# Hybrid encoder layer on one core: the order of weight loads, x1 stores, part sums and a memset in the last stage

## The reference, cut to what matters

```
xn = rms_norm(x);  q, k, v, u, g_attn, g_ssm = split(xn @ w_in)
attn_out = attention(rope(norm(q)), rope(norm(k)), v) @ w_attn_proj
y        = gelu(s5_bidirectional(u));  ssm_out = (y @ w_glu_a) * sigmoid(y @ w_glu_b)
x1 = x + (sigmoid(g_attn) * attn_out + sigmoid(g_ssm) * ssm_out) @ w_out
h  = rms_norm(x1)
out = x1 + square(relu(h @ w_ff1)) @ w_ff2          # w_ff1 1024 x 4096, w_ff2 4096 x 1024
```

## Time and profile before

| | |
|---|---|
| time, median of 3 runs | 2521.76 us (2520.86 to 2523.23) |
| the profiled execution: its own time | 2514.49 us |
| its span, first to last instruction | 2512.7 us |
| TensorE busy | 2473.1 us, 98% |
| VectorE, ScalarE, GpSimd busy | 1681.6, 1124.3, 1081.5 us |
| part one (three blocks) | from about 1083 to 1490 us |
| part two, first half; second half | to about 2004; to 2512 us |

### The profile page before, as it was taken

How to read it: one execution, slowest core, us unless ns; L and a number is a source line. 1 busy time by engine, 2 the same in 40 slices (tenths; PEclk the granted TensorE clock), 3 DMA queues, 4 the chain that set the end, 5 groups by cost and what they waited for, 6 DMA issues and landing times.

```text
span 2512.7 us, 37695 instructions
## 1 busy us (share of the span) xinstructions
PE 2473.1 (98%) x12320; PEld 2193.9 (87%) x12320; DVE 1681.6 (67%) x2349; ACT 1124.3 (45%) x1903; POOL 1081.5 (43%) x908
## 2 busy tenths in 40 slices
PE   8999999999999999999999989999999999999999
PEld 6888888888777777778787879999999999999999
DVE  7986688888888888876676766444446854444442
ACT  7554112121777777754444444333334343333341
POOL 0005664644667666654444423333333333333332
PEclk9999999999999999999999999999999999999999
DMA  5544232324552221144555633222222332222221
GB/s 184 178 161 168 87 98 82 94 81 108 139 121 70 51 64 44 38 158 151 193 193 197 223 133 135 68 68 68 68 68 94 122 132 69 70 70 68 68 68 67
DMA packets 160221, 271.29 MB, mean 108 GB/s; under 512 B 47184, under 2 KB 63056, under 8 KB 159952
## 3 DMA queue, kind: packets, MB, share of 16 engines
q1 hardware_dynamic: 160080, 269.46, 34.1%
HBM read 200.08 MB, written 59.24 MB: 103 GB/s over the span
## 4 chain that ended last, share of the span: by engine, by line
PE 91%; DVE 3%; DMA 2%; issue 1%; ACT 1%; SPq 1%; POOL 0%; DVEq 0%; ACTq 0%; POOLq 0%
PE banks L63 14%; PE banks L65 14%; PE banks L64 14%; PE banks L2859 6%; PE banks L2856 6%; PE banks L2858 6%; PE p_acc L63 3%; PE p_acc L65 3%; PE p_acc L64 3%; PE banks L1929 3%; PE banks L1928 3%; PE banks L1882 3%; PE banks L1877 3%; PE banks L1897 3%; PE banks L1876 3%; DMA t_wraw<-w_tail_t 2%
## 5 line engine op out<-in xcount | busy, mean ns | idle before, releaser
L63 PE MATMUL banks<-block,t_whi 128*128 128x384 f32 (+1 forms) x1088 | 387.8, 356 | 8.2 <-issue 5.7
L65 PE MATMUL banks<-block,t_wlo 128*128 128x384 f32 (+1 forms) x1088 | 386.6, 355 | 0.0
L1727 POOL TENSOR_TENSOR a_plo<-a_p,a_phi 128x512 fp32r<-128x512 f32 x239 | 308.8, 1305 | 141.1 <-DVE a_phi L1845 135.4
L2638 DVE TENSOR_TENSOR f_x<-banks,f_x 128x384 f32<-128x384 f32 x256 | 142.2, 557 | 293.1 <-PE banks L65 287.7
L64 PE MATMUL banks<-block,t_whi 128*128 128x384 f32 (+1 forms) x928 | 333.0, 359 | 0.0
L2856 PE MATMUL banks<-block,t_whi 128*128 128x384 f32 x800 | 268.7, 336 | 7.3 <-ACT f_snap L2503 5.4
L2859 PE MATMUL banks<-block,t_wlo 128*128 128x384 f32 x800 | 268.1, 335 | 0.0
L2385 POOL TENSOR_TENSOR t_wlo<-t_wraw,t_whi 128x1024 fp32r<-128x1024 f32 x67 | 164.3, 2453 | 229.2 <-ACT t_whi L2406 229.2
L2858 PE MATMUL banks<-block,t_whi 128*128 128x384 f32 x768 | 257.3, 335 | 0.0
L2390 POOL TENSOR_TENSOR t_wlo<-a_quotient,t_whi 128x512 fp32r<-128x512 f32 x96 | 141.8, 1477 | 224.4 <-ACT t_whi L2421 224.4
L1772 ACT ACTIVATE a_p<-banks 128x512 f32<-128x512 f32 x320 | 190.6, 596 | 95.8 <-PE banks L1929 86.8
(11 more groups left out here) (327 smaller groups left out, 6333.8 us busy)
## 6 DMA issues: line engine op xcount, KB each, us to landing
t_wraw<-w_tail_t SPq DMA_DIRECT2D x136, 512.0 KB, 4.2
a_quotient<-w_tail_t SPq DMA_DIRECT2D x64, 512.0 KB, 3.7
block<-roped_scratch SPq DMA_DIRECT2D x144, 128.0 KB, 2.8
w_raw<-w_in_t SPq DMA_DIRECT2D x31, 512.0 KB, 4.0
proj_scratch<-s_gate SPq DMA_DIRECT2D x48, 256.0 KB, 2.1
t_graw<-proj_scratch SPq DMA_DIRECT2D x24, 512.0 KB, 3.9
p_sw<-p_qn SPq DMA_DIRECT2D x60, 128.0 KB, 2.1
roped_scratch<-p_r_hi SPq DMA_DIRECT2D x30, 256.0 KB, 2.2
```

The lines of the kernel that those rows point to most:

```text
L63: pe.matmul(out, whi, xhi, start=start, stop=False)
L65: return pe.matmul(out, wlo, xhi, start=False, stop=stop)
L1727: pool.tensor_tensor(p_lo[s][:], p32[s][:], f32(p_hi[s][:]), ALU.subtract).then_inc(plo_pool, 1)
```

## The change

Six things, all in `tail`:

- SyncE: in the output projection tile loads are issued one step earlier. `next_w(b, S_2, 0)` stands ahead of the loop over m, `next_w` of m + 1 stands at the head of step m, the first `next_w` of the next block in step 7. The stores of x1 go one step later: tiles 0 to 5 behind steps 2, 4 and 6, tiles 6 and 7 in the next block's first step (or at the end).
- SyncE, last block: stage tiles 2 and 3 are loaded in steps 1 and 3 instead of 2 and 4, with a new wait for the stage tile before; weight units 2 and 3 in steps 6 and 7 instead of after the last store.
- VectorE: `rs` is cleared ahead of the last block's output projection too, and no longer at t = 2.
- VectorE: at the last block's m = 7 the low part of item 1 goes ahead of the fourth weight sum.
- VectorE: the second half's token parts are made in two portions per item, one ahead of the first eviction and one behind it; the sums can stop after each.
- ScalarE: at the items 168 and 344 (`group_at[h, 7]`) the last pair's results are split at the head of the step.

```diff
--- before.py
+++ after.py
@@ -2288,6 +2288,8 @@
                 view = stage_at(h, kt)[:].rearrange("p (k n) -> p k n", k=2)
                 rows = lambda t, n0, n1: t[kt:kt + KH + 1:KH, :, n0:n1].rearrange("k p n -> p k n")
                 if h == 0:
+                    if kt:
+                        st_in.wait(sp, 16 * kt)
                     sp.dma_start(view, rows(normed_d, 0, HALF)).then_inc(st_in.sem, 16)
                 else:
                     sp.dma_start(view[:, :, 0:2 * BLK - HALF], rows(normed_d, HALF, 2 * BLK)).then_inc(st_in.sem, 16)
@@ -2298,14 +2300,20 @@
                 mixed.wait(sp, 16 * h + 4 * (kt + 1))
                 mixed_lo.wait(sp, mixed_count(h, kt, 2))
 
+            def store_x1(b, i):
+                sp.wait_ge(x1_ready, b * KD + 2 * i + 4)
+                sp.dma_start(two_tiles(x1_d, b, i), x1[:, 2 * i:2 * i + 2]).then_inc(x1_out.sem, 16)
+
             for b in range(NBLK):
                 for m in range(KD):
                     for s in range(2):
-                        if not (b == 0 and m == 0 and s == 0):
+                        if (m, s) != (0, 0):
                             next_w(b, 2 * m + s, s)
                     if b == 0:
                         if m < 4:
                             load_x(0, m)
+                    elif m == 0:
+                        store_x1(b - 1, KD // 2 - 1)
                     elif m >= 4:
                         hn_out.wait(sp, 16 * (4 * (b - 1) + m - 2 if m < 6 else 4 * b))
                         load_x(b, m - 4)
@@ -2319,12 +2327,16 @@
                     if b == LAST and m == KD - 2:
                         hn_out.wait(sp, 16 * 4 * LAST)
                         load_stage(0, 0)
+                next_w(b, S_2, 0)
                 if b < LAST:
                     for s in range(2):
                         sp.wait_ge(st.attention[s], 16 * (NQ * NBLK // 2))
                     mix_chunk(b + 1, 0)
                 for m in range(KD):
-                    next_w(b, S_2 + m, m % 2)
+                    if m + 1 < KD:
+                        next_w(b, S_2 + m + 1, (m + 1) % 2)
+                    elif b < LAST:
+                        next_w(b + 1, 0, 0)
                     if b < LAST:
                         if m + 1 < N_MIX + 2:
                             mix_chunk(b + 1, m + 1)
@@ -2333,14 +2345,14 @@
                         load_stage(0, 1)
                         load_unit(0)
                         load_unit(1)
-                    elif m in (2, 4):
-                        stage_free(0, m // 2 - 1)
-                        load_stage(0, m // 2 + 1)
-                    if m % 2:
-                        sp.wait_ge(x1_ready, b * KD + m + 3)
-                        sp.dma_start(two_tiles(x1_d, b, m // 2), x1[:, m - 1:m + 1]).then_inc(x1_out.sem, 16)
-            load_unit(2)
-            load_unit(3)
+                    elif m in (1, 3):
+                        stage_free(0, m // 2)
+                        load_stage(0, m // 2 + 2)
+                    elif m >= KD - 2:
+                        load_unit(m - KD + 4)
+                    if m in (2, 4, 6):
+                        store_x1(b, m // 2 - 1)
+            store_x1(LAST, KD // 2 - 1)
 
             due = {}
             for r in range(4, len(feed.last_use)):
@@ -2488,9 +2500,24 @@
                             act.wait_ge(mix_in[m % 2], (b + 1) * 48 - 48 + (m // 2 + 1) * 16)
                             act.activation(chunk(m)[1], g_raw[m % 2][:], ACT.Copy).then_inc(mixhi_ready, 1)
 
+            def split_results(t):
+
+                for pg, i in a_parts(t, 0):
+                    r, c = a_order(pg)[i]
+                    h, p = divmod(pg, FF_PAIRS)
+                    if p >= 3:
+                        act.wait_ge(f2_done, 16 * (h * 8 + (p - 3) // 2 + 1))
+                    elif h:
+                        act.wait_ge(f2_done, 16 * 8)
+                    c_done.wait(act, 7 * pg + {(0, 1): 4, (1, 1): 5, (0, 0): 6, (1, 0): 7}[r, c])
+                    act.activation(act_cell(slot_of(pg), 0, r, c), ps[:, a_bank(pg, r, c), 0:QN],
+                                   ACT.Copy).then_inc(ahi_ready, 1)
+
             for t in range(3):
                 f_high(t)
             for t in range(END + 2):
+                if t in (feed.group_at[0, 7], feed.group_at[1, 7]):
+                    split_results(t)
                 for pg, d in feed.pairs_near(t, 1, 3):
                     h = pg // FF_PAIRS
                     if d == 1:
@@ -2516,16 +2543,8 @@
                         mix_high(1, kt, c)
                 if t + 3 < END:
                     f_high(t + 3)
-                for pg, i in a_parts(t, 0):
-                    r, c = a_order(pg)[i]
-                    h, p = divmod(pg, FF_PAIRS)
-                    if p >= 3:
-                        act.wait_ge(f2_done, 16 * (h * 8 + (p - 3) // 2 + 1))
-                    elif h:
-                        act.wait_ge(f2_done, 16 * 8)
-                    c_done.wait(act, 7 * pg + {(0, 1): 4, (1, 1): 5, (0, 0): 6, (1, 0): 7}[r, c])
-                    act.activation(act_cell(slot_of(pg), 0, r, c), ps[:, a_bank(pg, r, c), 0:QN],
-                                   ACT.Copy).then_inc(ahi_ready, 1)
+                if t not in (feed.group_at[0, 7], feed.group_at[1, 7]):
+                    split_results(t)
                 if t < 2:
                     for kt in (2 * t, 2 * t + 1):
                         mix_high(0, kt, T4)
@@ -2574,10 +2593,12 @@
                 if kt or h:
                     mixed_lo.wait(dve, 28 + 7 * kt if h else 6 * kt)
                 dve.tensor_tensor(t1, b12, b11, ALU.subtract).then_inc(mixed.sem, 1)
+                yield
                 mixed.wait(dve, n + 1)
                 dve.tensor_tensor(t2, b22, t1, ALU.subtract).then_inc(mixed.sem, 1)
                 yield
                 dve.tensor_tensor(t3, b22, b12, ALU.subtract).then_inc(mixed.sem, 1)
+                yield
                 mixed.wait(dve, n + 2)
                 if h and kt == 0:
                     c_done.wait(dve, 7 * FF_PAIRS)
@@ -2672,8 +2693,7 @@
                         for k in (2 * m - 2, 2 * m - 1):
                             dve.scalar_tensor_tensor(x1[:, k], x1[:, k], gn[:, k:k + 1], rs[:], ALU.mult,
                                                      ALU.mult).then_inc(hn_ready.sem, 1)
-                if b < LAST:
-                    dve.memset(rs[:], 0.0).then_inc(sq_step, 1)
+                dve.memset(rs[:], 0.0).then_inc(sq_step, 1)
                 dve.wait_ge(const_in, 32)
                 dve.wait_ge(x1_in, 16 * 4 * (b + 1))
                 for m in range(KD):
@@ -2692,12 +2712,12 @@
                         else:
                             for c in PREP[3:6]:
                                 quarter_low(0, kt, c)
-                        if m >= KD - 4:
-                            weight_sum(0, m - KD + 4)
                         if m == KD - 1:
                             for t in range(2):
                                 if feed.on_dve(t):
                                     f_low(t)
+                        if m >= KD - 4:
+                            weight_sum(0, m - KD + 4)
                     dve.wait_ge(summed, b * M_T + S_2 + m + 3)
                     dve.tensor_tensor(x1[:, m], ps[:, O_BANK + s], x1[:, m], ALU.add).then_inc(x1_ready, 1)
                     if b < LAST:
@@ -2709,7 +2729,30 @@
 
             if feed.on_dve(2):
                 f_low(2)
-            sums_of = None
+            sums_of = {kt: quarter_sums(1, kt) for kt in range(KH)}
+
+            def scale_new(kt, i):
+
+                if i == 0:
+                    st_in.wait(dve, 16 * KH + 32 * (kt + 1))
+                    dve.wait_ge(rs_ready, NBLK)
+                new = stage_at(1, kt)[:].rearrange("p (k n) -> p k n", k=2)[:, i, 2 * BLK - HALF:]
+                k = kt + KH * i
+                dve.scalar_tensor_tensor(new, new, gn[:, k:k + 1], rs2, ALU.mult, ALU.mult).then_inc(hn_ready.sem, 1)
+
+            def prepare(at, late_half):
+
+                if not 0 <= at < 16:
+                    return
+                kt, step = divmod(at, 4)
+                sums_now, lows = ((0, 1), (2, 1), (0, 0), (0, 0))[step][late_half], (
+                    ((), ()), ((), (B11,)), ((B22, B21), (T1,)), ((T2, T3), (T4,)))[step][late_half]
+                if step == 0:
+                    scale_new(kt, late_half)
+                for _ in range(sums_now):
+                    next(sums_of[kt], None)
+                for c in lows:
+                    quarter_low(1, kt, c)
             for t in range(END + 3):
                 if 0 < t <= END and feed.items[t - 1].kind == "f2":
                     evict(t - 1, 1)
@@ -2749,36 +2792,15 @@
                 if t in (1, 2):
                     for kt in (2 * t - 2, 2 * t - 1):
                         quarter_low(0, kt, T4)
-                if t == 2:
-                    dve.memset(rs[:], 0.0).then_inc(sq_step, 1)
```

(23 more changed lines are left out.)

## The result

| | before | after |
|---|---|---|
| median (lowest to highest) | 2521.33 us (2520.86 to 2523.23), 4 runs | 2496.14 us (2495.44 to 2503.57), 4 runs |
| ratio | | 0.991, 95% interval 0.9894 to 0.9925 |
| the profiled execution: time, span | 2514.49, 2512.7 us | 2496.11, 2494.3 us |

The change takes 25 us (1.0%) off the median. The prediction was 2503, range 2499 to 2512: the direction is right, the time lies 3 us under the range. Between the two traces the difference is only 18.4 us, and 18.9 had been predicted for that. So the working by stalls came out near for the trace, and the step from the trace to the median did not hold.

What follows compares the result with a forecast made beforehand. TensorE, busy 98% of the span, was taken as the bound, so only its stalls and low clock could be won. Gains of 4.5 + 3.6 + 5.5 + 3.9 + 1.4 = 18.9 us off 2521.8 gave 2503 us, range 2499 to 2512.

Steps and rivals of the forecast that it cites:

- the step from the trace to the median: Whole kernel: the gain of 18.9 us counted in the 2514.5 us trace was taken unchanged off the 2521.8 us median.
- part 1: Ends of the three blocks' output projections: weight tiles loaded ahead of x1 stores remove stalls, 4.5 plus 3.6 us.
- The price of a stall: TensorE's stalls: each costs its bracket plus some 0.15 us; low clock behind each of two long ones, 1.5 us.
- Tiles ahead of the stores: Output projections: earlier weight tile loads gain 4.5 us in the third block, 3.6 us at the ends of blocks one and two.
- 0.4 to 0.5 us too late for m=6: Third block's output projection: VectorE's addition of m=4 would end this much too late for TensorE's m=6.
- Items 0 to 20: Stretch to the last mean: early weight units 2 and 3 and memset gain 5.5 us, VectorE becoming the bound.
- Token parts and splits: Second half's preparation in two portions gains 3.9 us; splitting the last pair's results first gains 1.4 us.
- B: Rival: VectorE takes back more, before the mean and in the token parts' late halves; 2508 us, chance 0.17.
- C: Rival: early tiles come no earlier, as transfers set the time; only 2 of 8.1 us stay; 2509 us, chance 0.08.
- D: Rival: crowded transfers make at least five of 24 tiles land over 8.7 us after issue; 2528 us, chance 0.06.

Runs made afterwards that it cites:

- memset_only: The kernel before with only the memset of `rs` moved ahead of the output projection; 2518.08 us median, ratio 0.9994 to the kernel before.
- before_again: The kernel before, unchanged, run again for a second trace; 2515.75 us median over 10 runs.
- before_b: The kernel before, unchanged, run for a further trace; that trace took 2524.73 us.
- before_c: The kernel before, unchanged, run once more for another trace; that trace took 2515.3 us.
- sp_only: The kernel before with only SyncE's new order (tiles ahead of stores, weight units 2 and 3 early); 2503.98 us median, ratio 0.9934 to the kernel before.
- no_memset: The changed kernel with only the memset of `rs` put back at t = 2; 2500.9 us median, ratio 0.992 to the kernel before.
- old_parts: The changed kernel with the second half's token parts made as before, in one portion ahead of the first eviction; 2502.19 us median.
- no_sp: The changed kernel with SyncE's whole order as before; 2511.62 us median over nine runs, ratio 0.9968 to the kernel before.

## Why the prediction was wrong in its number, and where it was right

**The step that failed** is the one from the trace to the median: "the holes are the same work, so I take the same gain from it". For the profiled execution the prediction's figure was 2495.6 us and that execution took 2496.1. The median before lay 7 us over its trace, and these 7 us were taken to stay. They did not, and could not be counted on to, for two reasons that the runs show.

First, the holes are not the same work in each execution. In the old order a weight tile is asked for so late that a landing 1.2 us longer became a stall 1.25 us longer at the first tile and 2.5 us longer at the next (memset_only), and the low clock follows some of these stalls and not others. Six traces with the old order took 406.4 to 412.1 us to item 0, 408.2 in the mean; eight with the new order took 397.3 to 398.0. The first trace, 406.5, was among the shortest. So part 1 was worth 8.5 us between the two traces (4.5 + 3.6 = 8.1 predicted) and 10.4 us in the mean.

Second, the start of the last stage has two levels, 1083 to 1085 or 1090 to 1092 us, with any of these kernels (9 traces and 5). The change does not set it, but a few runs of each kernel can fall on unequal levels.

What the change is worth apart from such draws can be had in two ways. The means of the stretches differ by 10.4 + 5.4 + 5.8 + 0.5 = 22 us. The 54 runs of the kernel before on record (with before_again, before_b and before_c) have a median of 2518.2 us, the eight of the changed kernel one of 2495.8: 22.4 us. So of the 25 us measured some 22 are the change's, where 18.9 had been taken; the other 3 are the luck of the four runs that made the median before, 3 us above the 54. No trace exists of those four, so whether their 7 us over the first trace were the later level, longer stalls or both stays open. The range should have held an execution of average length.

**Term by term**, in the two first traces:
- The price of a stall was too low. From the matmul ahead of it to the fourth behind it, each of the five late-tile stalls of the trace before takes 0.24 to 0.25 us more than its bracket and the rhythm, not 0.15; the low clock behind the one at m=4 lasted 3.4 us at 0.5, which costs 1.7 us, not 1.5.
- Tiles ahead of the stores: 8.1 predicted, 8.5 measured. The four stalls and the one at m=4 went, and "0.4 to 0.5 us too late for m=6" is the 0.49 us of the trace.
- Items 0 to 20: 5.5 predicted, 5.6 measured, and VectorE became the bound as forecast: it worked from the addition of m=6 to the last squares without a gap, 21.9 us (1482.62 to 1504.49) against the 21.7 counted. TensorE's wait for it is 3.4 us at item 6; at the mean there is none, probably as the low clock had made item 6 slower (sp_only, without it, waits 0.8 us there). no_memset shows the memset's own share to be nothing, sp_only that SyncE's order alone wins all of it.
- Token parts and splits: 3.9 + 1.4 = 5.3 predicted, 5.7 + 0.5 = 6.3 measured (5.74 + 0.53). The halves took nearly every wait away (the waits for f_x are gone from the view above, where 1.0 us had been allowed for), and the first split is worth nothing by itself.
- Upstream, the stage began 2.0 us later in the trace after, which no part of the change touches (part of it is a low clock from 638.71 to 642.12 us, which the trace before has not): 20.4 less 2.0 is the 18.4 us between the traces.

Of the rivals, B and C did not come about: nothing beyond the counted work was taken back, and the tiles did come earlier. In part one, from 1095 us on, a tile lands in 3.8 us as a median where it took 4.5. For D, crowding: the longest landing is 6.5 us, under the 8.7 at which TensorE would stop, with three transfers in each step. Where the Trainium skill was cited (SBUF — State Buffer, "Who interferes with whom"), the trace agrees in the direction it shows: the weight sum at 1487.54 takes 1.78 us beside a subtraction of GpSimd that had started at 1487.22 and lasted 1.56 us, where such a sum alone takes 0.68. That GpSimd made TensorE wait in the new order was not seen.

## What to carry to other kernels

Before a gain read from one trace is taken off a median, place that trace among the kernel's runs: where a load sits so late that its landing time is on the path, the stall's size is a draw, and the trace shows one draw. In an issue queue that runs in order, put the load that only waits for a free buffer ahead of the store that waits for the newest result. And when a long wait is taken from an engine that then has work back to back, count that work: it gave 5.6 us here where 8 us of TensorE's stalls and a low clock had stood, and it left nothing for the memset or for most of a further spreading.

## What the runs showed of the hardware

The attention stage ahead of the last one runs at two speeds with the granted clock at 1.00 in both (1.00 is 2.4 GHz, 0.50 is 1.2). From 700 to 1070 us, TensorE's busy time, count of matmuls, clock, DMA share and GB/s: first before, then sp_only.

```profile
700.00:1070.00 370.00, 369.79 (x1595) 1.00 0.26 63
```

```profile
700.00:1070.00 370.00, 369.78 (x1568) 1.00 0.25 63
```

The slower one gets 27 matmuls less done in 370 us, 1.7%, which over that loop makes the 6 to 7 us between the two levels; after has 1595, before_b 1569. What sets the level was not tried.

The length of a stall did not decide whether the low clock followed. It came behind, or in the last part of, TensorE's stalls of 1.81 us (no_memset), 2.0 us (old_parts and memset_only), 2.68 us (no_sp) and nearly all of 2.9 us and more, and in after at 638.71 the last stall ahead of it, at 637.98, was one of 1.14 us. It did not come behind 2.03, 2.39 and 2.47 us in memset_only, 2.38 us in before_b, 1.88 us in sp_only, nor behind the 3.57 us at m=4 in before_again, where the granted clock is 1.00 from 1466 to 1480 us:

```profile
1466.44 0.47 PE L63 MATMUL banks<-block,t_whi 128*128 128x512 f32 x1 [3.57 <-issue]
```

In the last stage it lasted 3.4, 6.8 or 10.2 us at a time, at a granted clock of 0.50. The shortest costs up to 1.7 us of matmul time, less where TensorE stands still in it. What else decides was not tried. By these traces a stall of some 2 to 3.5 us costs its length and 0.25 us, and in some executions 1.7 us or more on top.
